# Where the weights' slots and the moving operands begin in SBUF: one layer of a hybrid decoder on one core

## The chip, the cores and the metric

The kernel runs on one core of one Trainium2 chip. The metric is the device time of one execution in microseconds. TensorE multiplies, VectorE (DVE), ScalarE (ACT) and GpSimd (POOL) work element by element, SyncE (SP) and GpSimd issue DMAs. SBUF has 128 partitions; an address is a byte within a partition.

## The reference

One step of a decoder layer for 256 prompt positions and 8 x 8 sampled ones with the same weights, 320 columns together, all in float32:

```
h = rmsnorm(x); z = h @ w_in                      # 2048 features
a, b = sparse attention, block-sparse attention   # over cached pages
c = retention (8 heads)
m = sig(gA)*(a @ w_pa) + sig(gB)*(b @ w_pb) + sig(gC)*(c @ w_pc)
x = x + m @ w_out
h2 = rmsnorm(x)
y = gelu(conv3(h2 @ ffn_up)) * (h2 @ ffn_gate)    # 5504 features
x = x + y @ ffn_down
return rmsnorm(x), the new keys, values and states
```

## The kernel before

Everything is kept with the features on the partitions: an operand of the dense products is a tensor of [128 partitions, K slices, 320 columns]. A dense product is done to nearly float32 precision from three products of a rounded format (float32r): every weight w and every operand x is split in a rounded part and a remainder, and w_hi x_hi, w_hi x_lo and w_lo x_hi are added in PSUM. The weights stand still in TensorE and are loaded anew for each matmul; the operand moves through it, 320 columns of it per matmul.

The dense work is a list of jobs (one block of 128 output features each), cut in units of up to 8 slices of 128 input features. There are 622 units. A unit's weights go through one of four slots (unit v uses slot v mod 4) of three buffers: SP brings them to `w_raw` (L436), ScalarE rounds them to `w_hi` (L1109), VectorE writes the remainders to `w_lo` (L1360), and TensorE uses them (L788 to L798), three matmuls per slice k, in the order (w_hi, x_hi), (w_hi, x_lo), (w_lo, x_hi). The same order of units is written out in every engine's program; the attention and retention steps stand between them at fixed places. Their first 1200 us hold both kinds of work, and from then on there is dense work nearly alone.

The operands are: `h_hi`, `h_lo` (16 slices; the normed input h, later the retention's output oc, later h2, all in the same place); `oa` and `ob` (8 slices each, the two attentions' outputs); `m` (16 slices); `y` (22 slices, refilled once with 21 for the second half of the features). In the trace, the products with h, oc and h2 all bear the name h.

Memory is laid out by hand. `Region` hands out places one behind the other, each rounded up to 32 bytes; `fix` is the region of what lives all through, and R, where it ends, is the start of the part that stages share. `at(a, b)` is a region between R+a and R+b. The program's first buffer, `ident`, begins at byte 16512; `h_hi` begins at 68736, `h_lo` at 89216, and R is 109696. A slot of weights has 8 x 128 x 4 = 4096 bytes, a slice of an operand 320 x 4 = 1280 bytes.

`ones`, a matrix of ones, is the stationary operand of the sums over features for the norms (L803, L809). ScalarE writes `m_hi` and `y_hi` slice by slice (L1118, L1127), VectorE `m_lo` and `y_lo` (L1444, L1466); `oa` and `ob` are split by one instruction each on both engines.

Of the kernel before, what the change touches and what calls it, by code (L numbers as in the profile page):

```python
# [7 lines left out]
ALU = mybir.AluOpType  # L8
ACT = mybir.ActivationFunctionType
F32 = mybir.dt.float32  # L10
F32R = mybir.dt.float32r
# [4 lines left out]
P = 128  # L16
# [3 lines left out]
T = TP + NS  # L20
KD = D // P
# [18 lines left out]
KU = 8  # L40
SLOTS = 4
LEAD = 3
SP_LEAD = 6
NBANK = 2

O_A, O_B, O_C = 0, 8, 16
KF1 = 22
# [79 lines left out]
S0 = 180  # L127


BEFORE = {"x": 0, "oc": 16, "oab": 32, "m": 34, "h2": 50, "y": 66}  # L130


# [22 lines left out]
def build(nc, a, out):  # L155

    ctx = ExitStack()
    with ctx:
# [32 lines left out]

        fix = Region(base, base + 93184)
        ident = fix("ident", [P, P])
        ones = fix("ones", [P, P])
        gmix, gffn, gfin = fix("gmix", [P, KD]), fix("gffn", [P, KD]), fix("gfin", [P, KD])
        rstd = fix("rstd", [P, T])
        pt_sb = fix("pt_sb", [1, NB * NPG], I32)
        w_raw = fix("w_raw", [P, SLOTS, KU * P])
        w_hi = fix("w_hi", [P, SLOTS, KU * P], F32R)

        epsc = fix("epsc", [P, 1])
        w_lo = fix("w_lo", [P, SLOTS, KU * P], F32R)
        fix("w_end", [P, 8])
        h_at = fix.at
        h_hi = fix("h_hi", [P, KD, T], F32R)
        h_lo = fix("h_lo", [P, KD, T], F32R)
        R = fix.at

        def at(start, end):
            return Region(R + start, R + end)  # L210


        r0 = at(0, 16704)
        qd = [r0(f"qd{m}", [P, NB, H, TS]) for m in "ab"]
# [75 lines left out]
        for i in range(2):  # L290
# [28 lines left out]
        pT = rg("pT", [P, 2, 4, P])  # L319
        vpg = rg("vpg", [P, V_LOTS, 2, 2, 256])  # L320
        ro = at(ring_at + 32, 109376)
        oa_hi, oa_lo = ro("oa_hi", [P, 8, T], F32R), ro("oa_lo", [P, 8, T], F32R)
        misc_at = ro.at - R
        ob_hi, ob_lo = ro("ob_hi", [P, 8, T], F32R), ro("ob_lo", [P, 8, T], F32R)
        x1_at = ro.at - R
        x1 = ro("x1", [P, KD, T])
        ost = at(x1_at, x1_at + 20480)("ost", [P, 2, 8, T])
        m_hi = at(0, 20480)("m_hi", [P, KD, T], F32R)
        m_lo = at(ring_at + 32, ring_at + 20512)("m_lo", [P, KD, T], F32R)
        rq = at(109376, 114496)  # L330
        sq = rq("sq", [P, 2, T])
        sqa = rq("sqa", [P, T])
        term = rq("term", [P, T])


        y_hi = at(0, 28160)("y_hi", [P, KF1, T], F32R)
        y_lo = at(28160, 56320)("y_lo", [P, KF1, T], F32R)
        rf = at(misc_at, x1_at)
        cw = rf("cw", [P, 4, KF])
        cst = rf("cst", [P, KF, 16])  # L340
        cend = rf("cend", [P, KF, 18])
# [52 lines left out]

        NPOOL = a["cache_a_k"].shape[1]
        W = {n: a[n] for n in ("w_in", "w_pa", "w_pb", "w_pc", "w_out", "ffn_up", "ffn_gate", "ffn_down")}
        X = {"h": (h_hi, h_lo), "oc": (h_hi, h_lo), "h2": (h_hi, h_lo), "oa": (oa_hi, oa_lo), "ob": (ob_hi, ob_lo),
             "m": (m_hi, m_lo), "y": (y_hi, y_lo)}
        z = (za, zb)

# [357 lines left out]
        def _(pe):  # L758
            mmul, turn = nc.tensor.matmul, nc.tensor.transpose
            at = 0  # L760
            last_in_bank = {}

            def dense(n):
                nonlocal at
                for _ in range(n):
                    x = UNITS[at]
                    job, q = x.job, job_bank(x.at)
                    if x.first:
                        if q in last_in_bank:
                            pe.wait_ge(bank_free, last_in_bank[q] + 1)  # L770
                        last_in_bank[q] = x.at
                    news = job.opens or job.second
                    if job.kind == "qi" and news:
                        pe.wait_ge(split, x.k0 + x.nk)
                    elif job.kind == "pc" and job.second:
                        pe.wait_ge(split, BEFORE["oc"] + x.k0 + x.nk)
                    elif job.kind in ("pa", "pb") and job.n == 0:
                        pe.wait_ge(split, BEFORE["oab"] + (1 if job.kind == "pa" else 2))
                    elif job.kind == "out" and news:
                        pe.wait_ge(split, BEFORE["m"] + x.k0 + x.nk)  # L780
                    elif job.kind == "up" and job.n == 0:
                        pe.wait_ge(split, BEFORE["h2"] + x.k0 + x.nk)
                    elif job.kind in ("d1", "d2") and news:
                        pe.wait_ge(split, BEFORE["y"] + job.wk + x.k0 + x.nk)
                    pe.wait_ge(w_lo_done, at + 1)
                    s = at % SLOTS
                    xh, xl = X[job.src]
                    for k in range(x.nk):  # L788
                        cols = slice(k * P, (k + 1) * P)

                        if job.kind == "ki":
                            pe.wait_ge(split, x.k0 + k + 1)
                        elif job.kind == "pc" and job.opens:
                            pe.wait_ge(split, BEFORE["oc"] + x.k0 + k + 1)
                        for t, (wp, xp) in enumerate(((w_hi, xh), (w_hi, xl), (w_lo, xh))):
                            mm = mmul(bank[q][:, 0:T], wp[:, s, cols], xp[:, x.k0 + k, :],  # L796
                                      start=(x.first and k == 0 and t == 0), stop=(x.last and k == x.nk - 1 and t == 2))
                    mm.then_inc(w_used, 1)  # L798
                    at += 1

            def sums(b, *src):
                for i, x in enumerate(src):
                    mm = mmul(bank[b][:, 0:T], ones[:, :], x, start=(i == 0), stop=(i == len(src) - 1))  # L803
                return mm

            pe.wait_ge(eps_set, 1)
            dense(5)
            pe.wait_ge(x_sqs, 1)
            mmul(bank[2][:, 0:T], ones[:, :], sqx[:, 0, :], start=True, stop=True).then_inc(n_sum, 1)  # L809
            dense(1)  # L810
            pe.wait_ge(r_in, 32)
            pe.wait_ge(eps_set, 2)
# [285 lines left out]
        def _(act):  # L1098
# [5 lines left out]
            def high(v):  # L1104
                if v >= SLOTS:
                    act.wait_ge(w_used, v - SLOTS + 1)
                act.wait_ge(w_arrived[v % SLOTS], 16 * (v // SLOTS + 1))
                n = UNITS[v].nk * P
                fn(w_hi[:, v % SLOTS, 0:n], w_raw[:, v % SLOTS, 0:n], ACT.Copy).then_inc(w_hi_done, 1)  # L1109

            def evacuated(j):
                job = JOBS[j]
                if job.kind == "sig":
                    act.wait_ge(bank_free, j + 1)
                    fn(sg[:, job.n % 4, :], sg[:, job.n % 4, :], ACT.Sigmoid).then_inc(sig_done, 1)
                elif job.kind == "pb":
                    act.wait_ge(m_done, job.n + 1)
                    fn(m_hi[:, job.n, :], m_f[:, job.n, :], ACT.Copy).then_inc(rounded, 1)  # L1118
                elif job.kind == "out":
                    act.wait_ge(bank_free, j + 1)  # L1120
                    if job.n == 0:
                        act.wait_ge(s_in, 80)
                    fn(h_hi[:, job.n, :], x1[:, job.n, :], ACT.Copy, scale=gffn[:, job.n:job.n + 1]).then_inc(rounded, 1)
                    squares(job.n, job.n)
                elif job.kind == "gate":
                    act.wait_ge(bank_free, j + 1)
                    fn(y_hi[:, job.n % KF1, :], yt[:, job.n % 2, :], ACT.Copy).then_inc(rounded, 1)  # L1127
                elif job.kind == "d2":
                    act.wait_ge(bank_free, j + 1)
                    squares(job.n, KD + job.n)  # L1130
                    fn(xg[:, job.n, :], x1[:, job.n, :], ACT.Copy, scale=gfin[:, job.n:job.n + 1]).then_inc(xg_done, 1)
# [204 lines left out]
            dense(6)  # L1336
            act.wait_ge(oab_in, 32)
            for m in range(2):
                fn((oa_hi, ob_hi)[m][:, :, :], ost[:, m, :, :], ACT.Copy).then_inc(rounded, 1)
            dense(UNIT_END["up", 0] - at)  # L1340
            act.wait_ge(n_sum, 2)
            fn(rstd[:, :], bank[2][:, 0:T], ACT.Sqrt, bias=epsc[:, :], scale=1.0 / D).then_inc(n_root, 1)
# [6 lines left out]
        def _(dve):  # L1349
# [7 lines left out]
            def low(v):  # L1357
                dve.wait_ge(w_hi_done, v + 1)
                n, s = UNITS[v].nk * P, v % SLOTS
                tt(w_lo[:, s, 0:n], w_raw[:, s, 0:n], w_hi[:, s, 0:n].bitcast(F32), ALU.subtract).then_inc(w_lo_done, 1)  # L1360

            def evacuate(j, end):
                job, psum = JOBS[j], bank[job_bank(j)][:, 0:T]
# [75 lines left out]
            def later(j):  # L1439
                job = JOBS[j]  # L1440
                n = job.n
                if job.kind == "pb":
                    dve.wait_ge(rounded, BEFORE["m"] + n + 1)
                    tt(m_lo[:, n, :], m_f[:, n, :], m_hi[:, n, :].bitcast(F32), ALU.subtract).then_inc(split, 1)  # L1444
                elif job.kind == "up":
                    u, c = ue[:, n % 2, :], cv[:, n % 2, :]
                    dve.wait_ge(ue_done, 2 * n + 2)
# [15 lines left out]
                elif job.kind == "gate":  # L1463
                    dve.wait_ge(rounded, BEFORE["y"] + n + 1)
                    i = n % KF1
                    tt(y_lo[:, i, :], yt[:, n % 2, :], y_hi[:, i, :].bitcast(F32), ALU.subtract).then_inc(split, 1)  # L1466

            def dense(n):
                nonlocal at
# [285 lines left out]
            dense(6)  # L1755
            for m in range(2):
                dve.wait_ge(rounded, BEFORE["oab"] + m + 1)
                tt((oa_lo, ob_lo)[m][:, :, :], ost[:, m, :, :], (oa_hi, ob_hi)[m][:, :, :].bitcast(F32), ALU.subtract)\
                    .then_inc(split, 1)
            dense(UNIT_END["up", 0] - at)  # L1760
            V(nc.vector.memset(ue[:, :, 0:2], 0.0))
            dve.wait_ge(n_root, 2)
# [141 lines left out]
```

## Time and profile before

| | |
|---|---|
| median of 3 runs | 2377.57 us (2377.52 to 2382.11) |
| the profiled execution | 2378.85 us |
| its span, first to last instruction | 2377.1 us |
| busy: TensorE, its weight loads | 2349.7, 2271.0 us |
| busy: VectorE, ScalarE, GpSimd | 1410.7, 919.4, 315.0 us |
| granted TensorE clock | 0.997 of 2.4 GHz |
| mean DMA rate | 193 GB/s |

The span is that of one execution; the time of that execution has a little more around it. A matmul's end is modelled in the profile, and matmuls overlap (one of 0.31 us begins every 0.14 us), so its pace is to be taken from start to start, or from a piece of the chain of waits divided by its count. Weight loads have rows of their own (PEld) and run beside the matmuls.

### The profile page before, as it was taken

To read this page: it belongs to the slowest core of one execution; us is meant where nothing else is said; L and a number is where in the kernel's file an instruction comes from. 1 tells how busy PE (TensorE), PEld (TensorE's weight loads), DVE (VectorE), ACT (ScalarE), POOL (GpSimd) and SP (SyncE) were. 2 spreads that over 40 slices of the span, in tenths; PEclk is the share of its full clock that TensorE was granted. 3 is DMA by queue.
4 is the path that set the end of the run, shared out by engine and by line. 5 is a ranking of instruction groups with operands and counts; after the bars stand their busy time and mean duration, and the time that the engine had idled before them with its cause. 6 is when DMAs were issued, how large, how long until landed. Compare 5 with 4: busy or idle time off the path is not lost.

```text
span 2377.1 us, 44497 instructions
## 1 busy us (share of the span) xinstructions
PE 2349.7 (99%) x17194; PEld 2271.0 (96%) x17202; DVE 1410.7 (59%) x2095; ACT 919.4 (39%) x1274; POOL 315.0 (13%) x629
## 2 busy tenths in 40 slices
PE   8999999999999999999999999999999999999997
PEld 8978999999999999999999999999999999999997
DVE  6545568899987545445456645666664356666443
ACT  5334443333343444334333344333333333333332
POOL 1135110000002322333200011000000000000001
PEclk9999999999999999999999999999999999999998
DMA  7447545546557988999775544444445544444553
GB/s 238 144 133 243 179 146 179 182 166 208 206 174 265 308 288 293 302 330 314 238 265 195 184 151 150 152 153 150 151 153 153 149 157 153 150 151 157 151 152 106
DMA packets 174434, 458.69 MB, mean 193 GB/s; under 512 B 25018, under 2 KB 74538, under 8 KB 174096
## 3 DMA queue, kind: packets, MB, share of 16 engines
q1 hardware_dynamic: 141040, 372.31, 46.6%
q0 software_dynamic: 26128, 75.67, 9.8%
q10 hardware_dynamic: 7056, 7.88, 0.9%
q8 instruction: 136, 2.23, 0.4%
q14 instruction: 74, 0.61, 0.1%
HBM read 425.27 MB, written 27.52 MB: 190 GB/s over the span
## 4 chain that ended last, share of the span: by engine, by line
PE 96%; DVE 1%; ACT 1%; issue 1%; DMA 1%; SPq 0%; DVEq 0%; ACTq 0%
PE ps L796 88%; PE ps L1068 1%; PE ps L1021 1%; PE ps L867 1%; PE ps L1051 1%; DMA kpg<-in_cache_a_k 0%; PE ps L991 0%; PE ps L934 0%; PE ps L983 0%; PE ps L879 0%; ACT w_hi L1109 0%; PE ps L974 0%; PE ps L970 0%; PE ps L831 0%; PE ps L909 0%
## 5 line engine op out<-in xcount | busy, mean ns | idle before, releaser
L1360 DVE TENSOR_TENSOR w_lo<-w_raw,w_hi 128x1024 fp32r<-128x1024 f32 (+1 forms) x622 | 749.4, 1207 | 773.8 <-ACT w_hi L1109 770.8
L796 PE MATMUL ps<-h_hi,w_hi 128*128 128x320 f32 x3696 | 1161.1, 314 | 9.3 <-DVE w_lo L1360 9.2
L796 PE MATMUL ps<-h_lo,w_hi 128*128 128x320 f32 x3696 | 1132.7, 306 | 0.0
L796 PE MATMUL ps<-h_hi,w_lo 128*128 128x320 f32 x3696 | 1126.2, 305 | 0.0
L1109 ACT ACTIVATE w_hi<-w_raw 128x1024 fp32r<-128x1024 f32 (+1 forms) x622 | 647.6, 1043 | 801.4 <-PE ps L796 786.3
L796 PEld LDWEIGHTS ps<-h_hi,w_hi 128*128 128x128 f32 x3696 | 695.1, 188 | 38.8 <-issue 36.5
L796 PEld LDWEIGHTS ps<-h_lo,w_hi 128*128 128x128 f32 x3696 | 695.3, 188 | 0.5
L796 PEld LDWEIGHTS ps<-h_hi,w_lo 128*128 128x128 f32 x3696 | 694.6, 188 | 0.0
L796 PE MATMUL ps<-y_hi,w_hi 128*128 128x320 f32 x688 | 213.3, 310 | 0.0
L796 PE MATMUL ps<-y_lo,w_hi 128*128 128x320 f32 x688 | 210.5, 306 | 0.0
L796 PE MATMUL ps<-y_hi,w_lo 128*128 128x320 f32 x688 | 209.2, 304 | 0.0
L796 PEld LDWEIGHTS ps<-y_lo,w_hi 128*128 128x128 f32 x688 | 129.2, 188 | 0.0
L796 PEld LDWEIGHTS ps<-y_hi,w_hi 128*128 128x128 f32 x688 | 129.2, 188 | 0.0
L796 PEld LDWEIGHTS ps<-y_hi,w_lo 128*128 128x128 f32 x688 | 129.1, 188 | 0.0
L691 POOL DMA_DIRECT2D vpg<-in_cache_b_v x128 | 69.1, 540 | 148.7 <-issue 73.7
L691 POOL DMA_DIRECT2D vpg<-in_cache_a_v x128 | 69.0, 539 | 125.8 <-issue 65.9
L796 PE MATMUL ps<-m_lo,w_hi 128*128 128x320 f32 x256 | 79.5, 310 | 0.0
L796 PE MATMUL ps<-m_hi,w_hi 128*128 128x320 f32 x256 | 78.9, 308 | 0.0
L738 POOL COPY cend<-ue 128x2 f32<-128x2 f32 x43 | 8.0, 187 | 532.0 <-DVEq L1426 532.0
L796 PE MATMUL ps<-m_hi,w_lo 128*128 128x320 f32 x256 | 78.2, 305 | 0.0
L1147 ACT ACTIVATE yv<-cv 128x320 f32<-128x320 f32 x43 | 20.3, 471 | 139.3 <-DVE cv L1459 139.3
L1490 DVE MAX8 top8b<-score 128x8 f32<-128x2056 f32 x32 | 73.4, 2295 | 0.0
(322 smaller groups left out, 2061.3 us busy)
## 6 DMA issues: line engine op xcount, KB each, us to landing
w_raw<-in_w_in SPq DMA_DIRECT2D x258, 512.0 KB, 4.9
w_raw<-in_ffn_up SPq DMA_DIRECT2D x86, 512.0 KB, 3.8
w_raw<-in_ffn_gate SPq DMA_DIRECT2D x86, 512.0 KB, 3.6
w_raw<-in_ffn_down SPq DMA_DIRECT2D x80, 448.0 KB, 3.3
kpg<-in_cache_b_k SPq DMA_DIRECT2D x128, 128.0 KB, 4.4
vpg<-in_cache_b_v POOLq DMA_DIRECT2D x128, 128.0 KB, 5.0
kpg<-in_cache_a_k SPq DMA_DIRECT2D x128, 128.0 KB, 4.5
vpg<-in_cache_a_v POOLq DMA_DIRECT2D x128, 128.0 KB, 5.1
```

Source lines behind the costliest of these rows:

```text
L691: pool.dma_start(vpg[:, lot % V_LOTS, s, j, :], a[("cache_a_v", "cache_b_v")[mx]][0] [bass.ds(page, 1)].rearrange("a p g d -> (a p) (g d)"))\
L738: nc.gpsimd.tensor_copy(cend[:, f, 0:2], ue[:, f % 2, 256:258]).then_inc(cend_done, 1)
L796: mm = mmul(bank[q][:, 0:T], wp[:, s, cols], xp[:, x.k0 + k, :], start=(x.first and k == 0 and t == 0), stop=(x.last and k == x.nk - 1 and ...
L867: mm = mmul(bank[b + g], flat(qi64[rows, p, :, :]), kix[rows, i % 4, :, :], start=True, stop=True)
L1021: mm = mmul(bank[2 + c][rows, :], flat(qd[mx][:, 2 * p + s, g * GRP:(g + 1) * GRP, :]), kpg[:, lot % K_LOTS, s, :, g, :], start=True, stop ...
L1051: mm = turn(bank[2 + c][:, j * P:(j + 1) * P], pr[:, (4 * c + j) * P:(4 * c + j + 1) * P], ident[:, :])
L1068: mm = mmul(bank[7][rows, 0:P], pT[:, j % 2, i, rows], vpg[:, lot % V_LOTS, s, i % 2, g * P:(g + 1) * P], start=(j == 0 and i == 0), stop= ...
L1109: fn(w_hi[:, v % SLOTS, 0:n], w_raw[:, v % SLOTS, 0:n], ACT.Copy).then_inc(w_hi_done, 1)
L1147: fn(yv[:, job.n % 2, :], cv[:, job.n % 2, :], ACT.Gelu).then_inc(g_done, 1)
L1360: tt(w_lo[:, s, 0:n], w_raw[:, s, 0:n], w_hi[:, s, 0:n].bitcast(F32), ALU.subtract).then_inc(w_lo_done, 1)
L1490: V(nc.vector.max(best[0:rows, :], vals))
```

## The change

The buffer `ones` becomes 8 columns wide, of which one is read 128 times over. A filler of 224 bytes goes ahead of `w_raw`. `w_hi` and `w_lo` become four tensors each, one per slot, with 32 and 64 bytes between them; `h_hi`, `h_lo` and R stay where they were. A new helper, `stepped`, places an operand in lots of slices, each lot beginning at a residue mod 256 that `STEPS` gives for its rounded part and its remainder: two lots for m, one each for oa and ob, three for y. What lies behind them moves by as much as needed. The instructions of TensorE, their order and the waits stay the same; they get their operands from lists by slice.

```diff
+HI_STEP, LO_STEP = 32, 64
+STEPS = {"m": (((0, 8), 96, 224), ((8, 16), 96, 128)),
+         "oa": (((0, 8), 64, 96),),
+         "ob": (((0, 8), 64, 128),),
+         "y": (((0, 8), 160, 224), ((8, 15), 0, 64), ((15, 22), 0, 128))}
+ROUND = 256
...
-        ones = fix("ones", [P, P])
+        ones = fix("ones", [P, 8])
...
+        fix("w_begin", [P, 56])
         w_raw = fix("w_raw", [P, SLOTS, KU * P])
-        w_hi = fix("w_hi", [P, SLOTS, KU * P], F32R)
-
+
+        def slots(name, step):
+
+            found = []
+            for i in range(SLOTS):
+                found.append(fix(f"{name}{i}", [P, KU * P], F32R))
+                if i + 1 < SLOTS and step:
+                    fix(f"{name}_end{i}", [P, step // 4])
+            return found
+
+        w_hi = slots("w_hi", HI_STEP)
         epsc = fix("epsc", [P, 1])
-        w_lo = fix("w_lo", [P, SLOTS, KU * P], F32R)
-        fix("w_end", [P, 8])
+        w_lo = slots("w_lo", LO_STEP)
...
+        def stepped(src, part, start, end):
+
+            by_k, by_lot = [], []
+            for (k0, k1), *steps in STEPS[src]:
+                start += (steps[part] - R - start) % ROUND
+                name = f"{src}_{('hi', 'lo')[part]}{k0}"
+                x = at(start, end)(name, [P, k1 - k0, T], F32R)
+                start += 4 * T * (k1 - k0)
+                by_k += [x[:, k, :] for k in range(k1 - k0)]
+                by_lot.append((k0, k1, x[:, :, :]))
+            return by_k, by_lot, start
...
-        oa_hi, oa_lo = ro("oa_hi", [P, 8, T], F32R), ro("oa_lo", [P, 8, T], F32R)
-        misc_at = ro.at - R
-        ob_hi, ob_lo = ro("ob_hi", [P, 8, T], F32R), ro("ob_lo", [P, 8, T], F32R)
-        x1_at = ro.at - R
-        x1 = ro("x1", [P, KD, T])
+        oa_hi, oa_hi_lots, end = stepped("oa", 0, ring_at + 32, 109376)
+        oa_lo, oa_lo_lots, misc_at = stepped("oa", 1, end, 109376)
+        ob_hi, ob_hi_lots, end = stepped("ob", 0, misc_at, 109376)
+        ob_lo, ob_lo_lots, x1_at = stepped("ob", 1, end, 109376)
+        x1 = at(x1_at, x1_at + 20480)("x1", [P, KD, T])
...
-        m_hi = at(0, 20480)("m_hi", [P, KD, T], F32R)
-        m_lo = at(ring_at + 32, ring_at + 20512)("m_lo", [P, KD, T], F32R)
+        m_hi, _, _ = stepped("m", 0, 0, 20832)
+        m_lo, _, end = stepped("m", 1, ring_at + 32, misc_at + 512)
...
-        y_hi = at(0, 28160)("y_hi", [P, KF1, T], F32R)
-        y_lo = at(28160, 56320)("y_lo", [P, KF1, T], F32R)
+        y_hi, _, y_mid = stepped("y", 0, 0, misc_at)
+        y_lo, _, _ = stepped("y", 1, y_mid, misc_at)
...
-                            mm = mmul(bank[q][:, 0:T], wp[:, s, cols], xp[:, x.k0 + k, :],
+                            mm = mmul(bank[q][:, 0:T], wp[s][:, cols], xp[x.k0 + k],
...
-                    mm = mmul(bank[b][:, 0:T], ones[:, :], x, start=(i == 0), stop=(i == len(src) - 1))
+                    mm = mmul(bank[b][:, 0:T], ones[:, 0:1].to_broadcast([P, P]), x, start=(i == 0), stop=(i == len(src) - 1))
```

## Rows read from the trace of the kernel before

**Rows 1.** The page: busy time of TensorE and its loads, the chain's shares.

```profile
PE 2349.7 (99%) x17194; PEld 2271.0 (96%) x17202; DVE 1410.7 (59%) x2095; ACT 919.4 (39%) x1274; POOL 315.0 (13%) x629
...
PE 96%; DVE 1%; ACT 1%; issue 1%; DMA 1%; SPq 0%; DVEq 0%; ACTq 0%
PE ps L796 88%; PE ps L1068 1%; PE ps L1021 1%; PE ps L867 1%; PE ps L1051 1%; DMA kpg<-in_cache_a_k 0%; PE ps L991 0%; PE ps L934 0%; PE ps L983 0%; PE ps L879 0%; ACT w_hi L1109 0%; PE ps L974 0%; PE ps L970 0%; PE ps L831 0%; PE ps L909 0%
```

**Rows 2.** The chain in order of time, longest pieces: start, length, what.

```profile
1027.02 10.28 DMA kpg<-in_cache_a_k
...
1217.92 254.06 PE ps L796 x1728
1472.52 887.50 PE ps L796 x6144
```

**Rows 3.** The chain in three stretches: with oa, with m, with h.

```profile
1238.72 56.46 PE ps L796 x385
...
1366.94 97.96 PE ps L796 x673
...
1479.90 280.23 PE ps L796 x1940
```

**Rows 4.** Matmul groups there: count, busy us, mean ns, idle; oa, m, h.

```profile
L796 PE MATMUL ps<-oa_lo,w_hi 128*128 128x320 f32 x128 | 39.5, 309 | 0.0
L796 PE MATMUL ps<-oa_hi,w_lo 128*128 128x320 f32 x128 | 39.5, 308 | 0.0
L796 PE MATMUL ps<-oa_hi,w_hi 128*128 128x320 f32 x128 | 39.4, 308 | 0.0
...
L796 PE MATMUL ps<-h_hi,w_hi 128*128 128x320 f32 x139 | 43.1, 310 | 0.0
L796 PE MATMUL ps<-h_lo,w_hi 128*128 128x320 f32 x139 | 42.5, 306 | 0.0
L796 PE MATMUL ps<-h_hi,w_lo 128*128 128x320 f32 x139 | 42.3, 304 | 0.0
```

**Rows 5.** Single instructions near 1600 us: start and length in us.

```profile
1599.92 0.31 PE L796 MATMUL ps<-h_lo,w_hi 128*128 128x320 f32 x1
1600.07 0.30 PE L796 MATMUL ps<-h_hi,w_lo 128*128 128x320 f32 x1
...
1599.93 0.19 PEld L796 LDWEIGHTS ps<-h_hi,w_lo 128*128 128x128 f32 x1
1600.07 0.19 PEld L796 LDWEIGHTS ps<-h_hi,w_hi 128*128 128x128 f32 x1
```

**Rows 6.** The page's groups of L796: count | busy us, mean ns.

```profile
L796 PE MATMUL ps<-h_hi,w_hi 128*128 128x320 f32 x3696 | 1161.1, 314 | 9.3 <-DVE w_lo L1360 9.2
...
L796 PE MATMUL ps<-y_hi,w_hi 128*128 128x320 f32 x688 | 213.3, 310 | 0.0
...
L796 PE MATMUL ps<-m_hi,w_hi 128*128 128x320 f32 x256 | 78.9, 308 | 0.0
```

**Rows 7.** Busy time by stretch, then clock, DMA share, GB/s.

```profile
core 0: us, PE busy (x) PEld busy (x) DVE busy (x) ACT busy (x) POOL busy (x), PEclk, DMA share, GB/s
1238.85:1295.16 56.31, 56.31 (x386) 56.31 (x385) 33.43 (x47) 16.97 (x16) 0.00 (x0) 1.00 0.58 194
1367.00:1464.80 97.80, 97.80 (x674) 97.80 (x673) 48.19 (x57) 41.45 (x58) 12.80 (x15) 1.00 0.43 151
1500.00:1560.00 60.00, 60.00 (x417) 60.00 (x417) 36.95 (x65) 21.69 (x26) 2.40 (x14) 1.00 0.45 153
378.00:768.00 390.00, 390.00 (x2801) 377.26 (x2797) 344.04 (x413) 148.94 (x198) 32.42 (x48) 1.00 0.58 198
768.00:1217.00 449.00, 447.36 (x4008) 415.50 (x4009) 218.69 (x348) 190.63 (x289) 134.92 (x247) 1.00 0.87 294
1472.50:2360.00 887.50, 887.50 (x6145) 887.25 (x6143) 484.19 (x768) 315.74 (x381) 35.32 (x143) 1.00 0.45 149
```

**Rows 8.** Loads of ones: count, ns (least, median, most).

```profile
L803 PEld LDWEIGHTS ps<-sqa,ones x4: 186/188/189, 1471.7 to 2361.3; 128*128 128x128 f32 x4
...
L809 PEld LDWEIGHTS ps<-sqx,ones x2: 187/188/188, 29.2 to 29.4; 128*128 128x128 f32 x2
```

**Rows 9.** Rounding and remainders of a unit of weights, by form.

```profile
L1360 DVE TENSOR_TENSOR w_lo<-w_raw,w_hi 128x1024 fp32r<-128x1024 f32 x542 | 662.0, 1224 | 634.2 <-ACT w_hi L1109 631.2
...
L1109 ACT ACTIVATE w_hi<-w_raw 128x1024 fp32r<-128x1024 f32 x542 | 571.5, 1057 | 676.7 <-PE ps L796 661.6 <-DMA w_raw<-in_w_in 9.1 <-DMA w_raw<-in_w_pc 5.0
```

More of the change, by code:

```diff
@@ L321, in build @@
         ro = at(ring_at + 32, 109376)
-        oa_hi, oa_lo = ro("oa_hi", [P, 8, T], F32R), ro("oa_lo", [P, 8, T], F32R)
-        misc_at = ro.at - R
-        ob_hi, ob_lo = ro("ob_hi", [P, 8, T], F32R), ro("ob_lo", [P, 8, T], F32R)
-        x1_at = ro.at - R
-        x1 = ro("x1", [P, KD, T])
+        oa_hi, oa_hi_lots, end = stepped("oa", 0, ring_at + 32, 109376)
[3 more added lines that the diff above has]
+        x1 = at(x1_at, x1_at + 20480)("x1", [P, KD, T])
         ost = at(x1_at, x1_at + 20480)("ost", [P, 2, 8, T])
-        m_hi = at(0, 20480)("m_hi", [P, KD, T], F32R)
-        m_lo = at(ring_at + 32, ring_at + 20512)("m_lo", [P, KD, T], F32R)
-        rq = at(109376, 114496)
+        m_hi, _, _ = stepped("m", 0, 0, 20832)
+        m_lo, _, end = stepped("m", 1, ring_at + 32, misc_at + 512)
+        rq = at(x1_at + 20480, x1_at + 25600)
         sq = rq("sq", [P, 2, T])
@@ L333, in build @@
         term = rq("term", [P, T])
-        y_hi = at(0, 28160)("y_hi", [P, KF1, T], F32R)
-        y_lo = at(28160, 56320)("y_lo", [P, KF1, T], F32R)
-        rf = at(misc_at, x1_at)
+        y_hi, _, y_mid = stepped("y", 0, 0, misc_at)
+        y_lo, _, _ = stepped("y", 1, y_mid, misc_at)
+        rf = at(misc_at + 512, x1_at)
         cw = rf("cw", [P, 4, KF])
@@ L396, in build @@
         W = {n: a[n] for n in ("w_in", "w_pa", "w_pb", "w_pc", "w_out", "ffn_up", "ffn_gate", "ffn_down")}
-        X = {"h": (h_hi, h_lo), "oc": (h_hi, h_lo), "h2": (h_hi, h_lo), "oa": (oa_hi, oa_lo), "ob": (ob_hi, ob_lo),
+        by_k = tuple([x[:, k, :] for k in range(KD)] for x in (h_hi, h_lo))
+        X = {"h": by_k, "oc": by_k, "h2": by_k, "oa": (oa_hi, oa_lo), "ob": (ob_hi, ob_lo),
              "m": (m_hi, m_lo), "y": (y_hi, y_lo)}
@@ L808, in _ @@
             pe.wait_ge(x_sqs, 1)
-            mmul(bank[2][:, 0:T], ones[:, :], sqx[:, 0, :], start=True, stop=True).then_inc(n_sum, 1)
+            mmul(bank[2][:, 0:T], ones[:, 0:1].to_broadcast([P, P]), sqx[:, 0, :], start=True, stop=True).then_inc(n_sum, 1)
             dense(1)
@@ L1108, in high @@
                 n = UNITS[v].nk * P
-                fn(w_hi[:, v % SLOTS, 0:n], w_raw[:, v % SLOTS, 0:n], ACT.Copy).then_inc(w_hi_done, 1)
+                fn(w_hi[v % SLOTS][:, 0:n], w_raw[:, v % SLOTS, 0:n], ACT.Copy).then_inc(w_hi_done, 1)
             def evacuated(j):
@@ L1117, in evacuated @@
                     act.wait_ge(m_done, job.n + 1)
-                    fn(m_hi[:, job.n, :], m_f[:, job.n, :], ACT.Copy).then_inc(rounded, 1)
+                    fn(m_hi[job.n], m_f[:, job.n, :], ACT.Copy).then_inc(rounded, 1)
                 elif job.kind == "out":
@@ L1126, in evacuated @@
                     act.wait_ge(bank_free, j + 1)
-                    fn(y_hi[:, job.n % KF1, :], yt[:, job.n % 2, :], ACT.Copy).then_inc(rounded, 1)
+                    fn(y_hi[job.n % KF1], yt[:, job.n % 2, :], ACT.Copy).then_inc(rounded, 1)
                 elif job.kind == "d2":
@@ L1338, in _ @@
             for m in range(2):
-                fn((oa_hi, ob_hi)[m][:, :, :], ost[:, m, :, :], ACT.Copy).then_inc(rounded, 1)
+                for k0, k1, x in (oa_hi_lots, ob_hi_lots)[m]:
+                    ins = fn(x, ost[:, m, k0:k1, :], ACT.Copy)
+                ins.then_inc(rounded, 1)
             dense(UNIT_END["up", 0] - at)
@@ L1359, in low @@
                 n, s = UNITS[v].nk * P, v % SLOTS
-                tt(w_lo[:, s, 0:n], w_raw[:, s, 0:n], w_hi[:, s, 0:n].bitcast(F32), ALU.subtract).then_inc(w_lo_done, 1)
+                tt(w_lo[s][:, 0:n], w_raw[:, s, 0:n], w_hi[s][:, 0:n].bitcast(F32), ALU.subtract).then_inc(w_lo_done, 1)
             def evacuate(j, end):
@@ L1443, in later @@
                     dve.wait_ge(rounded, BEFORE["m"] + n + 1)
-                    tt(m_lo[:, n, :], m_f[:, n, :], m_hi[:, n, :].bitcast(F32), ALU.subtract).then_inc(split, 1)
+                    tt(m_lo[n], m_f[:, n, :], m_hi[n].bitcast(F32), ALU.subtract).then_inc(split, 1)
                 elif job.kind == "up":
@@ L1465, in later @@
                     i = n % KF1
-                    tt(y_lo[:, i, :], yt[:, n % 2, :], y_hi[:, i, :].bitcast(F32), ALU.subtract).then_inc(split, 1)
+                    tt(y_lo[i], yt[:, n % 2, :], y_hi[i].bitcast(F32), ALU.subtract).then_inc(split, 1)
             def dense(n):
@@ L1757, in _ @@
                 dve.wait_ge(rounded, BEFORE["oab"] + m + 1)
-                tt((oa_lo, ob_lo)[m][:, :, :], ost[:, m, :, :], (oa_hi, ob_hi)[m][:, :, :].bitcast(F32), ALU.subtract)\
-                    .then_inc(split, 1)
+                for (k0, k1, lo), (_, _, hi) in zip((oa_lo_lots, ob_lo_lots)[m], (oa_hi_lots, ob_hi_lots)[m]):
+                    ins = tt(lo, ost[:, m, k0:k1, :], hi.bitcast(F32), ALU.subtract)
+                ins.then_inc(split, 1)
             dense(UNIT_END["up", 0] - at)
```

## The prediction, written before the change was run

> **What bounds the kernel now.** Read the page first [rows 1]: TensorE is busy 99% of a span of 2377.1 us and carries 96% of the chain that ended last, and one line, L796, has 88% of that chain. The chain in order of time [rows 2] says where: from 1472.52 us on, 6144 matmuls of L796 follow each other in one piece of 887.50 us, and before it 1728 in 254.06 us. Nobody is waited for there; the pace of a matmul is all there is. 14688 matmuls of that line (3 for each of 4896 products of a 128-row slice; the page has 3696 with h, 688 with y, 256 with m [rows 6], and oa and ob have 128 each [rows 4]) make 1 ns of pace worth 14.7 us.
>
> **The pace differs with the operand.** The chain of three stretches, each of one kind of operand [rows 3], gives start to start 280.23/1940 = 144.45 ns with h (and 887.50/6144 = 144.45 with h and y [rows 2]), 97.96/673 = 145.56 ns with m, 56.46/385 = 146.65 ns with oa. Shape, clock (granted 1.00, the 2.4 GHz level, in all of them [rows 7]) and line are equal. 320 columns at 2.4 GHz are 133.3 ns; so 11.1, 12.2 and 13.3 ns are lost in each. The groups of those stretches [rows 4] show inside them a second difference: with h the three matmuls of a product show 310, 306 and 304 ns, with oa 309, 308, 308. The single instructions [rows 5] show that the load of the next weights starts with each matmul and lasts 0.19 us, longer than the matmul's own share of the pace. So two reads of SBUF always run beside each other: the moving operand of one matmul and the weights of the next.
>
> What separates the three kinds is where they begin. A slice of moving operand has 1280 bytes, 5 times 256, one of weights 512 and a slot 4096; so a tensor keeps one residue mod 256 all through. Counting from the program's first buffer, ident at byte 16512, the residues are: rounded weights 64, remainders 96; h and y 128 in both parts; m 128 and 192; oa and ob 192 and 192. Take as distance D that of the moving operand's start from the start of the weights loaded beside it, mod 256. A product loads w_hi twice beside a hi part and w_lo once beside the lo part. D is then (64, 64, 32) for h and y, (64, 64, 96) for m, (128, 128, 96) for oa.
>
> **The rule that I take.** Let C(D) be the loss of a matmul. The three paces give, per product: 2C(64) + C(32) = 33.3 ns, 2C(64) + C(96) = 36.7, 2C(128) + C(96) = 40.0. So C(96) is 3.3 above C(32), and C(128) 1.7 above C(64); one number is free. With C(64) = 11.67 the four lie on a ramp: 10.0, 11.67, 13.33, 13.33 at 32, 64, 96, 128. I choose this, as the even one, and continue it as its mirror image round the circle, for which no row speaks: 11.67 at 160, 10.0 at 192, 8.33 at 224 and 0. 8.33 is also what the cheapest matmul inside the steady pattern of h shows: 304 ns beside 310 and 306; their mean of 306.7 belongs to a pace of 144.45, so 304 belongs to 141.8 [rows 3, 4].
>
> **The change, part by part.** ident, ones (480 bytes shorter), a filler of 224 and the slots' pads sum up so that h stays at byte 68736. New residues by slot: rounded weights 64, 96, 128, 160; remainders 192, 0, 64, 128.
> - h (3696 products; also oc and h2): D with w_hi is 64, 32, 0, 224 by slot, with w_lo 192, 128, 64, 0. Loss per product 33.3, 33.3, 28.3, 25.0, mean 30.0 against 33.3: 3696 x 3.33 ns = 12.3 us less.
> - m (256): first lot at 96 and 224, in slots 0 and 2: D 32 and 224, with w_lo 32 and 160: 30.0, 28.3. Second at 96 and 128, in slots 1 and 3: 0 and 192, with w_lo 128 and 0: 30.0, 28.3. Mean 29.2 against 36.7: 1.9 us less.
> - oa (64 and 96) and ob (64 and 128), 128 each: D with w_hi 0, 224, 192, 160; both means come to 30.0 against 40.0: 2.6 us less together.
> - y (688), lots at 160/224, 0/64, 0/128: 32.5, 35.0 and 35.0, weighted by 8, 7 and 7 slices 34.1 against 33.3: 0.5 us more.
> Sum: 12.3 + 1.9 + 2.6 - 0.5 = 16.3 us less.
>
> What hides some of it: of the h products 2256 lie before 1217.9 us (6816 matmuls less 48 of a start with other work, divided by 3). In 378 to 768 us VectorE is busy 344.04 of 390 us [rows 7], yet the chain goes through TensorE there, so that I count the gain in full. In 768 to 1217 us, with 96 units of 8 products, the pages of the caches arrive at 294 GB/s, and the chain holds a piece of 10.28 us of waiting for kpg [rows 2]; there I give back half of 768 x 3.33 ns: 1.3 us. Left: 15.0 us.
>
> Edits costed at nothing: ones read with a step of nought as weights, 8 matmuls and loads of L803 and L809, whose loads take 188 ns like any [rows 8]; were each load to double, 8 x 0.19 = 1.5 us more; less than nothing is excluded, as they do no less. The rounding and the subtraction write into slots at other residues: 1057 and 1224 ns per unit [rows 9] beside 24 x 144.45 = 3467 ns of matmuls. The remainders at 96 and the rounded at 64 are the only rows for this; bounds are a tenth faster or slower, both covered. The oa and ob rounding is still one instruction a lot. No wait, queue or DMA is added or moved. The unit's supply has to keep up with 3440 instead of 3467 ns; the stage after 1472 us uses 484.19 of 887.50 us of VectorE.
>
> The profiled execution takes 2378.85 us, 1.75 around the span; less 15.0 is 2363.9. The median of the runs is 1.3 lower, so 2362.6.
>
> Bounds of the rule: the cheapest residues everywhere (8.33) and the dearest of the rows everywhere (13.33) give 14688 x (141.7 - 144.5) = -41 us and 14688 x (146.7 - 144.5) = +32 us.
>
> The Trainium skill, SBUF — State Buffer, "Who interferes with whom", gives TensorE two independent read ports and says that PE and ACT never wait on anyone. By that the places would not matter, and the paces of 144.45 and 146.65 ns at one shape and clock [rows 3] are not explained by it; which of the two holds for slots apart decides rival 1.
>
> **Rivals.**
> 1. Place does not matter: what separates m and oa from h is something else of their stretches (VectorE is busy for 33.43 of 56.31 us beside oa, 48.19 of 97.80 beside m, 36.95 of 60 beside h [rows 7]: near 0.6, 0.5 and 0.6, which does not order them). Against it: the pattern inside a product is as steady as the operand. Time: 2377.6. Chance 0.12.
> 2. Slower: the plateau goes on. Of the free circle nothing is known, and 13.33 may stand at all D but 32 and 64. Then three of four slots with h lose their good place: 36.7, 33.3, 38.3, 40.0, mean 37.1; 3696 x 3.75 = 13.9 us more; m 37.5 and 0.2 more, oa and ob 0.1 less, y 36.7, 39.6 and 39.6, 3.6 us more. Together +17.5: 2395. It decides as soon as C(0) and C(224) together are over 22.5 ns (16.7 in the forecast), all else kept. For it: the rows show C flat from 96 to 128. Chance 0.17.
> 3. All places off the ramp are at the cheapest, and changing slots keeps the reads apart: 25.0 ns per product. 8.33 x 4384 for h and y, 11.7 x 256, 15 x 256: 43.4 us less, 2334. For it: 304 ns in the steady pattern. Against: new slots pass over 32 to 160 as well. Chance 0.13.
> 4. The gain counts only where TensorE waits for nobody: before 1217.9 us VectorE (0.88 busy in 378 to 768 us) and the pages take it back. 2256 x 3.33 = 7.5 us of the 16.3 go: 2378.85 - 8.8 - 1.3 = 2368.8. Against: the chain names TensorE there too. Chance 0.12.
>
> **How the numbers follow.** My forecast has 0.46 and by itself holds 2354 to 2371. A measurement tells 0.2%, 4.8 us, from no change. Forecast, rivals 3 and 4 are faster, 0.71, less 0.02 for what of them comes within 4.8 us: 0.69. Same: 0.12 and a little, 0.13. Slower: 0.18. The range takes in rival 3's neighbourhood and most of the way to rival 2: 2336 to 2388.
>
> **What would show it.** In one steady stretch with h2 the durations must differ from slot to slot with a period of four units, where they are all 310, 306, 304 now; the mean pace there must be near 143.3 ns, with m near 143.1, oa and ob near 143.3, y near 144.7. Rival 1: 144.45 in all. Rival 2: 145.7 with h. Rival 3: 141.7 everywhere. Rival 4: 143.3 in every stretch, but the waits of L796 before 1217 us grow by some 7 us. The whole is wrong if neighbouring matmuls carry over more to each other than a sum over D can hold; the uneven 310, 306, 304 of one product, with D 64, 32, 64, are a warning of that.

## The result: 27 us slower, and the profile after

The changed kernel takes 2404.87 us (2404.13 to 2406.66, 4 runs), the one before 2377.91 us beside it: a ratio of 1.0112, interval 1.0100 to 1.0124. The prediction was 2362.6 us, with a range of 2336 to 2388: the wrong side, and outside the range. Beside one of the later runs a single execution of the kernel before took 6030 us in a slow state; it is left out of every comparison.

In the page of the changed kernel, the line of busy times that answers to [rows 1], then the chain's pieces that answer to [rows 2] (start, length, what; L825 is the line of the dense matmuls now):

```profile
PE 2375.8 (99%) x17194; PEld 2296.4 (96%) x17202; DVE 1410.9 (59%) x2095; ACT 919.2 (38%) x1274; POOL 314.2 (13%) x629
...
1195.37 287.10 PE ps L825 x1944
1483.01 902.31 PE ps L825 x6144
```

The busy time of VectorE and ScalarE moved by 0.2 us, that of TensorE by 26.1. The last 6144 matmuls take 902.31 instead of 887.50 us and begin 10.5 us later: 14.8 and 10.5 are the whole of the 25.3 us by which the span grew. Nobody waits longer: the wait of the dense line for the remainders of weights is 9.0 us, as it was 9.2 [rows 6]. The chain in the stretches of [rows 3], in the order oa, m, h2, and behind them one with y:

```profile
1248.06 56.48 PE ps L825 x385
...
1376.27 99.03 PE ps L825 x673
...
1489.93 290.20 PE ps L825 x1975
...
1786.17 193.85 PE ps L825 x1322
```

Length by count gives 146.70, 147.15, 146.94 and 146.63 ns from start to start, where oa had 146.65, m 145.56, h2 and y 144.45. So all operands run at about the pace that oa had alone; h2 and y lost the 2.2 to 2.5 ns that they had been better by, and h and oc, in the part before with other work between, lost 1.7 ns. Inside h2 the pace goes by slot. Four units of 24 matmuls, slots 0 to 3 in this order:

```profile
1638.04 3.49 PE ps L825 x24
1641.53 3.57 PE ps L825 x24
1645.10 3.52 PE ps L825 x24
1648.62 3.53 PE ps L825 x24
```

From start to start, all matmuls of h2 have means by slot of 145.49, 148.79, 146.67 and 146.80 ns (24 matmuls in 3.49 us are 145.4, in 3.57 us 148.8). In the kernel before, all four had 144.45.

### The profile page after: what moved, and what is told of

Its sections match the earlier page's. It is cut to its first block, busy times and chain, and to the rows that moved or that the text cites. A ratio compares the mean times of both kernels' runs of the same rounds, so it can differ in the third digit from the quotient of the medians.

```text
span 2402.4 us, 44497 instructions
## 1 busy us (share of the span) xinstructions
PE 2375.8 (99%) x17194; PEld 2296.4 (96%) x17202; DVE 1410.9 (59%) x2095; ACT 919.2 (38%) x1274; POOL 314.2 (13%) x629
## 4 chain that ended last, share of the span: by engine, by line
PE 97%; DVE 1%; ACT 1%; issue 0%; DMA 0%; DVEq 0%; ACTq 0%
PE ps L825 89%; PE ps L1097 1%; PE ps L1050 1%; PE ps L896 1%; PE ps L1080 1%; PE ps L1020 0%; PE ps L963 0%; PE ps L1012 0%; PE ps L908 0%; PE ps L1003 0%; PE ps L999 0%; ACT w_hi L1138 0%; PE ps L860 0%; PE ps L938 0%; PE ps L992 0%
## 5 line engine op out<-in xcount | busy, mean ns | idle before, releaser
L825 PE MATMUL ps<-h_hi,w_hi 128*128 128x320 f32 x3696 | 1156.0, 313 | 9.1 <-DVE w_lo L1391 9.0
L825 PE MATMUL ps<-h_lo,w_hi 128*128 128x320 f32 x3696 | 1142.4, 309 | 0.0
L825 PE MATMUL ps<-h_hi,w_lo 128*128 128x320 f32 x3696 | 1141.8, 309 | 0.0
L825 PEld LDWEIGHTS ps<-h_hi,w_hi 128*128 128x128 f32 x3696 | 695.0, 188 | 38.9 <-issue 36.9
L825 PEld LDWEIGHTS ps<-h_lo,w_hi 128*128 128x128 f32 x3696 | 695.9, 188 | 0.4
L825 PEld LDWEIGHTS ps<-h_hi,w_lo 128*128 128x128 f32 x3696 | 694.8, 188 | 0.0
L825 PE MATMUL ps<-y_hi,w_lo 128*128 128x320 f32 x688 | 212.7, 309 | 0.0
L825 PE MATMUL ps<-y_hi,w_hi 128*128 128x320 f32 x688 | 212.6, 309 | 0.0
L825 PE MATMUL ps<-y_lo,w_hi 128*128 128x320 f32 x688 | 212.4, 309 | 0.0
L825 PEld LDWEIGHTS ps<-y_hi,w_hi 128*128 128x128 f32 x688 | 129.3, 188 | 0.0
L825 PEld LDWEIGHTS ps<-y_hi,w_lo 128*128 128x128 f32 x688 | 129.3, 188 | 0.0
L825 PEld LDWEIGHTS ps<-y_lo,w_hi 128*128 128x128 f32 x688 | 129.3, 188 | 0.0
L720 POOL DMA_DIRECT2D vpg<-in_cache_b_v x128 | 68.9, 538 | 151.1 <-issue 73.7
L825 PE MATMUL ps<-m_hi,w_lo 128*128 128x320 f32 x256 | 79.3, 310 | 0.0
L825 PE MATMUL ps<-m_hi,w_hi 128*128 128x320 f32 x256 | 79.3, 310 | 0.0
L825 PE MATMUL ps<-m_lo,w_hi 128*128 128x320 f32 x256 | 79.3, 310 | 0.0
```

What stands on the lines that cost most here:

```text
L720: pool.dma_start(vpg[:, lot % V_LOTS, s, j, :], a[("cache_a_v", "cache_b_v")[mx]][0] [bass.ds(page, 1)].rearrange("a p g d -> (a p) (g d)"))\
L825: mm = mmul(bank[q][:, 0:T], wp[s][:, cols], xp[x.k0 + k], start=(x.first and k == 0 and t == 0), stop=(x.last and k == x.nk - 1 and t == 2))
```

## Experiments

The theory that stood after the result: the four residues that were there before (h 128, its remainder 128, rounded weights 64, remainders of weights 96; a set is written in this order from here on) were an unusually good set, and what counts is not a sum of two distances but how one matmul's reads leave things for the next. Its rival was the prediction's own sum over distances with other numbers in it.

**grid.** The matmuls alone. The core of it, in place of the layer:

```diff
+            for i, (h, l, p, q) in enumerate(todo):   # 512 sets: q, l, h over 0..224 in steps of 32, p = 64
+                for k in range(16):
+                    j = k % 8
+                    ...                               # hi, lo, w1, w2: slice j at its residue
+                    for t, (w, x) in enumerate(((w1, hi), (w1, lo), (w2, hi))):
+                        nc.tensor.matmul(ps[:, i % 8, 0:T], w, x, start=(k == 0 and t == 0), stop=(k == 15 and t == 2))
```

> The reads measured by themselves: nothing but matmuls, in blocks of 16 products (48 matmuls in the order rounded weights x rounded operand, rounded weights x remainder, remainder weights x rounded operand), with no other engine at work and no slots. Rounded weights stand at residue 64 mod 256; the rounded operand, its remainder and the remainder weights take each of the eight residues in steps of 32 bytes: 512 blocks. It leaves out the whole layer. Theory 'a sum over distances' (the prediction's rule): a product's time is 400 ns plus 2C(hi - w_hi) plus C(lo - w_lo), so that the 512 means are explained by 8 + 8 numbers to within 0.5 ns of pace, and C(0) and C(224) come out above 11 ns each. Theory 'carry-over': which of the four residues stand together matters, a sum over two distances leaves over 1 ns of pace unexplained in many blocks. Both: the block at 128, 128, 96 has the 144.45 ns of the kernel before, 128, 192, 96 has 145.6 and 192, 192, 96 has 146.7, with no other engine at work. If these three do not come back, it is other engines' accesses that set the pace, and the residues are innocent.

The chain over four blocks of 48 matmuls: the sets of h, m and oa in the kernel before, and one at the slow end (192, 96, 64, 128):

```profile
1624.68 6.96 PE ps L211 x48
...
1736.96 6.99 PE ps L211 x48
...
1751.04 7.04 PE ps L211 x48
...
2032.69 7.23 PE ps L211 x48
```

By the starts of the last 36 matmuls of a block: 144.44, 145.56, 146.67 and 151.11 ns. The three paces of the layer are back within 0.02 ns, with no other engine at work. Over the 512 sets the mean is 146.71, the least 144.36, the most 151.11, and most values (432 of 512 within 0.1 ns) stand on a ladder with steps of 1.11 ns; 284 of the sets are at 146.67, 35 under 144.5. So the set of before is at the lower end, and a set taken blindly costs 2.2 ns more. A sum over the two distances with 16 free numbers, fitted to all 512, leaves 0.97 ns of the spread (standard deviation) of 1.03 ns, and is off by over 1 ns in 119 sets: it explains next to nothing. Nor would another way of joining the two distances help much: a free number for each of their 64 pairs leaves 0.91 ns.

**slots_only and lots_only.** The two halves of the change.

```diff
 slots_only
-STEPS = {"m": (((0, 8), 96, 224), ((8, 16), 96, 128)), "oa": (((0, 8), 64, 96),), ...
+STEPS = {"m": (((0, 8), 128, 192), ((8, 16), 128, 192)), "oa": (((0, 8), 192, 192),), ...   # all as before
 lots_only
-HI_STEP, LO_STEP = 32, 64
+HI_STEP, LO_STEP = 0, 0
+        fix("w_end", [P, 72])          # behind w_lo: h stays where it is
```

> The changed kernel with m, oa, ob and y back at the residues that they had before (128/192, 192/192, 192/192, 128/128); only the slots stay apart by 32 and 64 bytes. Theory 'the slots do it': the products with h, 11088 of 14688 matmuls, lose 2.0 ns each, 22 us, and y loses with them: 2398 to 2406 us. Theory 'the lots do it': under 2385 us.

> The changed kernel with its slots back beside each other (rounded weights 64, remainders 96 in every slot, as before); only m, oa, ob and y begin at their new residues. Products with h must be back at 144.45 ns. Theory 'a sum over distances' gives m 5.0, oa 15.0 and ob 13.3 ns less per product and y 0.2 less, 5 us in all: 2373 us. Theory 'carry-over' gives no number ahead of the grid; whatever comes must be what the grid shows for the same four residues.

slots_only: 2403.76 us, ratio 1.0107 (1.0091 to 1.0124), all but 1 us of the loss. lots_only: 2384.06 us, 1.0026 (1.0016 to 1.0036), 6 us on its own: h2 is at 144.45 ns again, y at 146.4, 147.9 and 146.4 in its three lots, m at 146.8 and 147.1, oa at 146.7, ob at 147.3. The sum over distances gave 2373 for it and is refuted here too. The two losses don't add (25.8 and 6.1 are more than 27.0), since with the slots apart y is near the blind mean already, with old lots (146.3) or new (146.7). The grid has 147.78 for the second lot of y and for ob, 146.67 for the third of y and for m and oa, which the layer shows within 0.5 ns; for the first lot of y it has 144.44 where the layer has 146.4. That miss asked for grid2.

**hi_only and lo_only.** One step each, everything else at the old residues.

```diff
 hi_only
-HI_STEP, LO_STEP = 32, 64
+HI_STEP, LO_STEP = 32, 0               # remainders of weights at 96 in every slot
 lo_only
-HI_STEP, LO_STEP = 32, 64
+HI_STEP, LO_STEP = 0, 64               # rounded weights at 64 in every slot
```

> Operands all at their old residues, remainder weights at 96 in every slot; only the rounded weights' slots are 32 bytes apart (64, 96, 128, 160). Slot 0 has the old set. Theory 'the old set is one lucky lock, any other set runs at the grid's mean of 146.7': h and y at 144.44 in slot 0 (perhaps after a few products), 146.7 in slots 1 to 3; 13152 x 0.75 x 2.25 = 22 us more: 2400 us. Theory 'a sum over distances' fitted to the grid: no more than 146.7 - 144.4 in any slot either, but the same in each product.

> Operands and rounded weights at their old residues; only the remainders' slots are apart (192, 0, 64, 128), so that no slot has the old set. Theory 'any other set runs at the grid's mean': 146.7 in all four slots, 13152 x 2.25 = 30 us more less what the grid gives for the four sets (146.67, 145.92, 146.67, 145.19 for remainders at 192, 0, 64, 128: mean 146.1, 22 us): 2400 to 2408 us.

hi_only: 2396.88 us (2 runs), 1.0081 (1.0062 to 1.0099), where 2400 was said; h2 by slot 144.62, 146.56, 146.38, 146.08. The slot that kept the old set kept its pace, the others fell to near the mean. lo_only: 2394.32 us (2 runs), 1.0070 (1.0051 to 1.0088), less than the 2400 that I had as the lower end; but the pattern is as the grid has it: 145.54, 145.63, 146.91, 145.24 against 145.56, 145.92, 146.67, 145.19. My slip was one of reading: the grid has 145.56 and not 146.67 for remainders at 192, so that its mean over the four sets is 145.83 and 13152 matmuls make 18 us, 2396 us in all. Most of the remaining 2 us goes with h before 1472 us, where the pace rose by 1.2 ns only, against 1.4 in h2.

**grid2.** Does a set have one pace?

> Matmuls alone again, without the layer. (a) 16 sets of four residues, each in 8 blocks of 16 products in shuffled order: does a set have a pace, or does the state in which the block before left TensorE choose it? Theory 'carry-over' in its strong form: several sets show two or more paces, all on a ladder with steps of 1.11 ns (144.44, 145.56, 146.67, ...); the sets of the kernel before show theirs in most of 8. Theory 'a set has a pace': one value per set, within 0.1 ns. (b) the set 128, 128, 64, 96 with all four moved by the same 32 to 224 bytes and by 4, 8, 16: if only the places towards each other matter, all of them run at 144.44. (c) both parts at one distance D from weights of one residue: 146.67 at most D, by the first grid. (d) 120 sets drawn in steps of 4 bytes: mean near 146.7, least 144.4. (e) units of 8 products that go through the changed kernel's four slots: mean near 146.9 as in the changed kernel with h2; units of 8 at one place 144.44; long blocks of 64 hold their pace to the end.

(a) Nine of the 16 sets had one pace in all 8 blocks, within 0.2 ns, the old set 144.44 eight times; seven had two or more, most of them steps of the ladder. Of these, the changed kernel's slot 1 (128, 128, 96, 0) had 145.6 five times and 148.78 three times, and the first lot of y of lots_only (160, 224, 64, 96) had 144.4 to 144.6 six times and 147.78 twice. Two blocks of the one set of slot 1:

```profile
73.99 6.99 PE ps L225 x48
...
88.12 7.15 PE ps L225 x48
```

The addresses in SBUF are the same in both. What differs is the block ahead and the bank of PSUM (block i writes bank i mod 8), and the bank is not it: in bank 0 the set had 145.61 ns once and 148.78 once. So what ran before chooses between two steady patterns. The name of the set ahead does not always tell which: (160, 224, 64, 96) had 144.53 and 147.78 behind two blocks of the same set (128, 128, 64, 192). One block of 64 products of slot 1's set held its pattern (145.5 to 145.6) to its end. (b) The old set with all four residues moved by 16 or by any multiple of 32 bytes stays at 144.4 to 144.75; moved by 4 bytes it is at 150.9, by 8 at 148.8, where 144.44 was expected if only the places towards each other mattered. With the rounded operand alone moved it is worse for 16 bytes too: 146.6 to 146.75. (c) With one distance for both pairs the pace is 146.67 at every one of the eight distances: a loss of 13.33 ns, and the distance by itself counts for nothing. (d) 120 sets in steps of 4 bytes: mean 147.9, where 146.7 was expected, least 144.42. Among 632 sets in all none is under 144.3. (e) The changed kernel's slots, unit by unit, without the layer:

```profile
2371.89 3.49 PE ps L225 x24
2375.38 3.57 PE ps L225 x24
2378.95 3.52 PE ps L225 x24
2382.47 3.53 PE ps L225 x24
```

These are the four rows of the changed kernel above, to the hundredth of a microsecond (145.50, 148.79, 146.71, 146.79 ns). Behind slot 0, slot 1 landed in its slower pattern in all eight rounds.

**all_128.** The old slots, and m, oa, ob at 128 like h.

```diff
-STEPS = {"m": (((0, 8), 96, 224), ((8, 16), 96, 128)), "oa": (((0, 8), 64, 96),), "ob": (((0, 8), 64, 128),), ...
+STEPS = {"m": (((0, 8), 128, 128), ((8, 16), 128, 128)), "oa": (((0, 8), 128, 128),), "ob": (((0, 8), 128, 128),), ...
```

> Slots beside each other as before, and m, oa, ob moved to 128 in both parts, where h and y are: the set 128, 128, 64, 96 for every product. Theory 'this set is a good one wherever it is used': m falls from 145.6 to 144.44, oa and ob from 146.7, together 768 x 1.1 + 768 x 2.3 = 2.6 us less than before: 2375.3 us. Theory 'what is faster with h and y is their stretch, not their place': 2377.9 us.

2376.14 us against 2377.98, ratio 0.9993 (0.9984 to 1.0002): the interval just reaches no change. The paces did what was said: oa 144.45, m 144.6, ob 144.9 instead of 146.9 (its steps over 160 ns left out); the chain's pieces are

```profile
1217.00 252.35 PE ps L826 x1728
1469.89 887.49 PE ps L826 x6144
```

with the last one as in [rows 2] and the one ahead of it, which holds oa, ob and m, 252.35 instead of 254.06 us. This is the best layout found; it is 1.8 us under the kernel before by the medians.

**lo_192.** A number given ahead for a layout that only the grid had seen.

```diff
-HI_STEP, LO_STEP = 32, 64
+HI_STEP, LO_STEP = 0, 0                # w_lo begins at residue 192 in every slot, operands as before
```

> A number given ahead from the grid, for a layout that was not run in the layer: operands and rounded weights at their old residues, the remainders at 192 in every slot. The block 128, 128, 64, 192 had 145.56 ns in 8 of 8 blocks: h and y at 145.56 instead of 144.44, 13152 x 1.11 = 14.6 us; m from 145.56 to 146.67 (block 128, 192, 64, 192), 0.9 us; oa and ob stay at 146.67: 2393.4 us, h and y without a difference between slots. If the layer's other work decided, there is no reason for 145.56.

2390.54 us, 1.0053 (1.0035 to 1.0070). h2 is at 145.55 in all four slots, y at 145.4 to 145.8, m at 146.7, as the grid said. oa is at 144.45 instead of 146.67, and ob near it at 145.0, another set with two patterns it seems; that is 1.7 of the 2.9 us that the number was too high.

**grid3.** Which of the two reads is it?

```diff
+                    if mode == "w0":
+                        w1, w2 = w1[:, 0:1].to_broadcast([P, P]), w2[:, 0:1].to_broadcast([P, P])
+                    if mode == "x0":
+                        hi, lo = hi[:, 0:1].to_broadcast([P, 320]), lo[:, 0:1].to_broadcast([P, 320])
```

> Matmuls alone, third set. (w0) the same blocks of 320 columns, but the weights loaded are one element read 128 times, so that the load sweeps over no addresses; (x0) the weights as before, but the moving operand one element read 320 times. Theory 'the two reads get into each other's way': in both modes the pace no longer depends on the set, and falls well below the 144.4 ns that no set went under, toward 133.3 ns and a few more. Theory 'one read alone sets the loss by where it begins': one of the two modes keeps the differences between the sets. (widths) the sets of before, of oa, of m and the changed kernel's four slots at 128, 256, 384 and 512 columns: if it is the two reads that meet, the loss per matmul is of like size at 256 to 512 columns, since a load of 128 columns is then over before the matmul is, and the sets differ there too. (units) the changed kernel's own sequence of sets unit by unit for y, m, oa and ob must give its paces: y 147.0, m 147.2, oa 146.7, ob 146.5 (without its waits), each within 0.5 ns, and y of the kernel with the old slots 146.9.

The chain over a block with the weights read in one place (w0, set of oa), and over one with the moving operand read in one place (x0, same set):

```profile
25.77 7.03 PE ps L231 x48
...
46.37 6.52 PE ps L231 x48
```

The first block of a run is left out; its first matmuls begin 267 ns apart. x0: 135.83 ns in each of the three sets, 2.5 over the 133.33 of 320 columns. w0: 146.67 in each of them. So the larger loss needs a moving read that goes through addresses; with it standing still only 2.5 ns are left, in these sets, with the load reading as before. With the load standing still the loss is there, but it no longer depends on the set: the first theory expected it to fall in both modes, and it fell in one. The Trainium skill, TensorE: Matmul & The Clock Gate, "Back-to-back issue gap", has N / 2.4 + 2.5 ns as the gap of an isolated warm matmul, and says that in a stream of loads and matmuls both set the spacing. By that formula 320 columns are an estimated 135.8 ns: x0 agrees with it, and the layer's 144.45 and 146.67 do not.

By width: 117.6 to 118.8 ns at 256 columns, 173.3 to 175.6 at 384, 230.9 to 233.3 at 512, a loss of 11 to 12, 13 to 16 and 18 to 20 over the columns at 2.4 GHz; at 128 columns 111.6 in all sets. I had expected a loss of like size at 256 to 512 columns; it grows with the matmul. The order of the sets changes with the width as well: the set of oa is as fast as the old one at 384 (173.33 both) and the slowest of the seven at 512 (233.33 against 231.11). The units of the changed kernel gave y 146.56, m 147.15, oa 146.66, and y of lots_only 146.99, within 0.5 ns of what was said; ob gave 145.46 where 146.5 was said. The layer's own ob, its steps over 160 ns left out, is at 145.7, so the number said ahead was off.

**grid4.** Is it the meeting with the load that costs?

```diff
-                    w1 = wh[:, p // 4 + 128 * j:p // 4 + 128 * j + 128]
+                    w1 = wh[:, p // 4 + 128 * j:p // 4 + 128 * j + m]        # m = 32, 64, 96, 128
```

> Matmuls alone, 320 columns, seven sets (before, oa, m, the changed kernel's four slots), but the weights are 32, 64, 96 or 128 columns wide: the load beside a matmul sweeps over 128, 256, 384 or 512 bytes and the moving read stays whole. The third set of blocks had left open why the loss grows with the matmul's width (17.8 ns at 512 columns, 11.1 at 256), although the load beside is of the same size. Theory 'each meeting with the load costs': the loss over 133.3 ns falls with the load's length, to 2.5 to 6 ns at 32 columns, and the sets come together. Theory 'a moving read that sweeps has a loss of its own, which a load only shifts': above 144 ns at 32 columns of weights too.

The groups of a block with 32 columns of weights (set of m); a load now takes 108 ns instead of 188:

```profile
L220 PE MATMUL ps<-xh,wl 128*32 128x320 f32 x17 | 5.2, 307 | 0.0
...
L220 PEld LDWEIGHTS ps<-xh,wl 128*32 128x32 f32 x16 | 1.7, 108 | 0.6
```

The pace stays: 144.44 to 146.72 over the seven sets at 32 columns (the first block again left out), 145.5 to 147.8 at 64 and 96, 144.44 to 148.8 at 128. Which set is good changes with the width (the old one has 146.67, 147.78, 147.78, 144.44 at 32, 64, 96, 128). The first theory is refuted: a quarter of the load costs as much as the whole. What is shown is that a sweeping moving read has the loss, and that the load's place and length move it by some ns up or down. Why a sweeping read has it stays open.

## Why the prediction was wrong

- **Where the time is.** Right: TensorE's pace in the dense line is the whole of it, and no wait, queue or other engine took part. VectorE and ScalarE need 1224 and 1057 ns per unit at the new places as at the old [rows 9], the loads of ones 188 ns [rows 8]; the edits costed at nothing cost nothing.
- **That the places set the pace.** Right, and rival 1 is out: with one shape and nothing else running the grid has 144.4 to 151.1 ns when only residues (and with them the block ahead) change, and hi_only and lo_only slow the layer by moving weights alone. Whether the two reads share anything no run tells; that the matmul's pace does not depend on where the weights lie, as the prediction took it from the Trainium skill, SBUF — State Buffer, "Who interferes with whom", is refuted.
- **"Let C(D) be the loss of a matmul."** This is the step that failed. The loss is not a sum over distances. Three measured paces were fitted by four numbers, so nothing could contradict them; the even ramp through them and its mirror image were invention. With one distance in both pairs, C is 13.33 ns at all eight D (grid2, c), where the ramp had 8.33 to 13.33; the pace goes with all four residues together and with what ran before (grid2, a). The prediction had also left out a row of its own: by [rows 5] a load lasts 0.19 us and the next one begins 0.14 later, so that a matmul has parts of two loads beside it, and one distance per matmul covers one. The sign followed from the ramp: the ramp's cheap end at 0, 192 and 224 made me expect 30.0 ns per product with h, where the mean over four slots is 146.94 x 3 - 400 = 40.8.
- **The operands, part by part.** h, -12.3 us by the sum: measured 4128 x 2.49 = +10.3 in h2, and 6960 x 1.7 = +11.8 with h and oc, whose mean pace went from 144.66 to 146.36 ns. m -1.9: it is 768 x 1.6 = +1.2. oa and ob -2.6: between 0 and -0.3. y +0.5: it is 2064 x 2.2 = +4.5. Together that is 27.6 us, and the span grew by 25.3. Some of it hid before 1483 us, where other work stands between: the steps of over 200 ns from a dense matmul to the next matmul sum to 55.4 us there, where they had 58.2. The prediction had given back 1.3 us for this.
- **Rival 2** had the right side and 2395 us, not its mechanism: its good places at 32 and 64 don't exist either. What it could have said is that h and y, the cheapest of three kinds, stood at a good set and another might be nearer to the dearest. That oa's 146.65 is the mean over sets taken blindly (146.71) only the grid shows; three paces could not tell it. Moving every set without a reason that the trace bears out is a draw from that distribution: 13152 matmuls of h and y times 2.2 ns give an estimated +29 us, and h and y lost 26.6.
- **The warning** at the end (310, 306, 304 ns beside D of 64, 32, 64) was the true reading: two matmuls with the same distance had durations 6 ns apart, and in the grid's block of that set their starts are 148 and 142 ns from the next, which no function of D can give. It should have cost the forecast its first place.

What stays open: by which rule a set and a state give a pattern. The ladder of 1.11 ns is a 3.33 ns step per product of three matmuls; a shift of all four residues of the old set by 16 bytes changes nothing, by 4 or 8 much; the runs say no more. That one set of addresses can run in two paces, and that a repeated sequence repeats its pace (slot 1 in eight rounds of eight), is shown. That it is TensorE's reads that carry something over is argued, and what they would carry is not known.

## What to carry to other kernels

Where a long run of float32r matmuls is the bound, its start-to-start pace is worth measuring for the layout itself, in a small kernel with nothing but the matmuls: it gave the layer's four unit times to 0.01 us. Keep one set of residues that has been measured at the width in use for every slot and operand (16-byte starts at least), and bring other operands to it, instead of spreading slots; here that kept the old pace, and the 1.8 us that all_128 gained are not clear of the noise. Measure a set behind several others, since one block can show the better of two paces. And a rule with as many free numbers as the profile has values is no rule: look for a pair of rows that it could fail on, such as two matmuls of equal cause and unequal time.

## What the runs showed of the hardware that I had not expected

- A float32r matmul of 320 columns with its weights loaded anew takes 144.4 to 151.1 ns by where the four operands of its product begin mod 256 (in steps of 32 bytes), and 135.83 if the moving operand is read in one place.
- One set can have two steady paces, 145.6 and 148.8 ns for (128, 128, 96, 0), chosen by what ran before and not by the bank of PSUM, kept over a whole block of 48 matmuls.
- The paces of h2, in both kernels, are the same with the rest of the layer at work and without: VectorE, ScalarE and DMAs on the same memory made no difference of 0.1 ns. Other operands differ from the grid's single blocks by up to 2.2 ns (y's first lot, oa in lo_192), which goes with the sets that have two paces.
- Loads of 32 columns instead of 128 (108 against 188 ns) do not make the matmuls beside them faster.
